# A conditioned decoder layer: the input projection in three rounded products, and key norms taken on strips

## What is computed

```python
h = modulate(x, norm_mix_w, shift1, scale1)
c_q, c_kv, k_rope, slab, gate_a, gate_b = _split(h @ w_in, IN_SIZES)
...
p = p + (prev - p) * rwkv_mu            # prev: the slab of the token before
r, k, v, w_lo, a_lo, g_lo = _split(p, ...)
log_w = -softplus(-(w0 + tanh(w_lo) @ w2)) - 0.5
a = sigmoid(a0 + a_lo @ a2)
g = sigmoid(g_lo) @ g2
kk = heads(k * k_k)
kk = kk / maximum(sqrt(sum(kk * kk, axis=-1)), 1e-12)
k = k * (1.0 + (a - 1.0) * k_a)
```

## Time and profile before

| | us |
|---|---|
| median of three runs | 1730.0 |
| lowest and highest | 1729.05, 1730.19 |
| span of the profiled execution | 1726.8 |
| median less that span | 3.2 |
| `phase_project`, first to last PE matmul | 47.3 to 180.1 |
| the other mixer blocks | 181.2 to about 605 |

### The profile page before, as it was taken

How to read it: one execution, slowest core, us unless ns; L and a number is a source line. 1 busy time by engine, 2 the same in 40 slices (tenths; PEclk the granted TensorE clock), 3 DMA queues, 4 the chain that set the end, 5 groups by cost and what they waited for, 6 DMA issues and landing times.

```text
span 1726.8 us, 44239 instructions
## 1 busy us (share of the span) xinstructions
PE 1664.4 (96%) x18700; PEld 875.8 (51%) x18700; DVE 613.7 (36%) x1421; ACT 412.9 (24%) x849; POOL 279.1 (16%) x349
## 2 busy tenths in 40 slices
PE   8999897899999988999999999999999999999997
PEld 5444796466488973344344344334334434434433
DVE  3679474753234554122122122213213213212212
ACT  3142333555123221121121111111112112112111
POOL 5000530101000011121121221221221221221121
PEclk8999999999999989999999999999999999999999
DMA  9950000401221288999999999999999999999993
GB/s 358 346 206 1 2 5 15 166 1 50 86 109 50 98 310 330 370 395 403 381 408 402 390 401 402 388 398 402 391 393 403 396 390 408 399 389 405 401 361 132
DMA packets 98221, 489.64 MB, mean 284 GB/s; under 512 B 15100, under 2 KB 17209, under 8 KB 48838
## 3 DMA queue, kind: packets, MB, share of 16 engines
q1 hardware_dynamic: 88012, 470.76, 68.9%
q0 software_dynamic: 7504, 16.80, 4.1%
q10 hardware_dynamic: 2636, 1.08, 0.3%
HBM read 478.61 MB, written 19.55 MB: 288 GB/s over the span
## 4 chain that ended last, share of the span: by engine, by line
PE 61%; DVE 1%; issue 0%; ACT 0%; POOLq 0%; DVEq 0%; ACTq 0%
PE bank L2131 38%; PE bank L2142 19%; PE bank L2122 1%; PE bank L2155 1%; PE bank L2143 1%; PE bank L2132 1%; PE bank L2170 0%; PE bank L2165 0%; DVE sb_y L2353 0%; DVE sb_biased L2334 0%; POOLq L2023 0%; ACT sb_xT L2222 0%; DVE sb_bias_part L2367 0%; DVE sb_mod L2344 0%; DVE sb_xT L2324 0%
## 5 line engine op out<-in xcount | busy, mean ns | idle before, releaser
L2131 PE MATMUL bank<-sb_w_raw,sb_xT 128*32 128x512 f32 x4608 | 668.0, 594 | 2.5 <-ACT sb_xT L2222 1.4
L2132 PE MATMUL bank<-sb_w_raw,sb_xT 128*32 128x512 f32 x1536 | 667.5, 594 | 0.0
L2131 PEld LDWEIGHTS bank<-sb_w_raw,sb_xT 128*32 128x32 f32 x4608 | 186.1, 110 | 450.1 <-issue 446.6
L2142 PE MATMUL bank<-sb_w_raw,sb_aT 128*32 128x256 f32 x4608 | 337.9, 379 | 2.0 <-DVE sb_aT L2331 2.0
L2143 PE MATMUL bank<-sb_w_raw,sb_aT 128*32 128x256 f32 x1536 | 337.5, 380 | 0.0
L2334 DVE TENSOR_TENSOR sb_biased<-bank,sb_bias 128x512 f32<-128x512 f32 x96 | 60.3, 683 | 608.8 <-PE bank L2132 537.3
L2142 PEld LDWEIGHTS bank<-sb_w_raw,sb_aT 128*32 128x32 f32 x4608 | 187.7, 110 | 130.8 <-DVE sb_y L2353 2.3
L2233 ACT COPY sb_bias<-sb_last_quarter 32x1536 f32<-32x1536 f32 x32 | 47.0, 1467 | 501.6 <-POOL sb_last_quarter L2290 501.6
L2143 PEld LDWEIGHTS bank<-sb_w_raw,sb_aT 128*32 128x32 f32 x1536 | 166.3, 110 | 0.0
L2132 PEld LDWEIGHTS bank<-sb_w_raw,sb_xT 128*32 128x32 f32 x1536 | 166.2, 110 | 0.0
L2285 POOL TENSOR_TENSOR sb_tick<-sb_ones 128x1 f32<-128x1 f32 x93 | 34.8, 374 | 571.9 <-DVE sb_y L2353 223.2
(11 more groups left out here) (456 smaller groups left out, 2110.5 us busy)
## 6 DMA issues: line engine op xcount, KB each, us to landing
sb_w_raw<-in_w_gate_up_dram SPq DMA_DIRECT2D x256, 1024.0 KB, 17.8
sb_w_raw<-in_w_down_dram SPq DMA_DIRECT2D x128, 1024.0 KB, 19.1
sb_ring<-in_w_in_dram SPq DMA_DIRECT2D x7, 2048.0 KB, 11.1
sb_x<-in_ada_w_dram SPq DMA_DIRECT2D x8, 1024.0 KB, 8.7
sb_mod<-in_ada_w_dram SPq DMA_DIRECT2D x8, 1024.0 KB, 9.1
sb_ring<-in_ada_w_dram SPq DMA_DIRECT2D x3, 2048.0 KB, 12.8
sb_x<-in_x_dram SPq DMA_DIRECT2D x2, 2048.0 KB, 11.0
sb_ring<-in_w_out_dram SPq DMA_DIRECT2D x2, 2048.0 KB, 8.5
```

The source lines that it names most:

```text
L2131: te.matmul(up_bank[r][at, :], g.xT[:, k, at], g.w_raw[:, s, 512 * r:512 * r + 512], start=first, stop=last)
L2132: mm = te.matmul(up_bank[r][CAP:P, :], g.xT[:, k, STRIP * r:STRIP * r + STRIP], g.w_raw[:, s, 512 * G:2048], start=first, stop=last)
L2142: te.matmul(down_bank[j][at, 0:256], g.aT[:, k, at], g.w_raw[:, s, 1024 * r + 256 * j:1024 * r + 256 * j + 256], start=first, stop=last)
```

## The change

The projection's products are made of rounded float32, as the gates' are now. Of `g.hT` and of each weight tile a high part (rounded) and a low part (the rest) are kept, and each product is three: high by high, high by low, low by high.

- `phase_adaln`: hidden features go to `g.h32` (over `g.AR`), the normalised tokens to `g.mod` in place of `xn`. GpSimd, after its constants, splits the first chunk (two copies, two subtractions). SP issues the first two late half chunks here, behind the chunk loads.
- `phase_project`: DVE and ACT round four tiles of the hidden state each; DVE subtracts for the eight low parts. For each of the twelve r, k and v tiles ACT writes the high part into one of three buffers, and GpSimd writes the low part over the raw weights in the ring; ACT and GpSimd do the same for the attention's inputs in one piece of 128 by 3328. The first two outputs do their low-hidden products last.
- Key norms: the sums of squares go to four strips of 32 partitions of one bank (16 matmuls), one square root, one maximum and one reciprocal of 128 by 128, and 16 matmuls spread them back to four banks (rn). ss and rn stand ahead of v in TensorE's list, g behind m. The decays of the first two tiles stand ahead of the norm on DVE.
- `phase_output`: the two ACT casts and two DVE subtractions of `g.hT` go. The low parts, written to DRAM at the end of the projection's SP list, come back by two 1 MB loads, and GpSimd copies them (4 copies of 128 by 1024) before ga.
- Buffers move: `phase_mla` has its v tokens in `g.gate` and its q and k in `g.AR`.

```diff
+def low_slot(g, i):
+
+    k, n = g.chunks[i].shape[1:]
+    return g.ring_r[:, i % RING, 0:k * n].rearrange("p (k n) -> p k n", k=k)
...
+def late_place(g, h):
+    buf = (g.x, g.mod)[h // 2]
+    return buf[:, 2 * (h % 2):2 * (h % 2) + 2, :].rearrange("p a (b n) -> p (a b) n", n=512)
...
+            sp.wait_ge(*act.at(f"xn{NT - 1}"))
+            for h in range(2):
+                sp.dma_start(late_place(g, h), ada_chunk(a, 4, 512 * h, 512 * h + 512)).then_inc(g.late_in[h], 16)
...
+            pool.wait_ge(*chunk_loaded(g, LO))
+            for i in range(2):
+                pool.tensor_copy(g.first_hi[:, i], slot(g, LO)[:, :, P * i:P * i + P]).then_inc(*first(f"hi{i}"))
+            for i in range(2):
+                pool.wait_ge(*first.at(f"hi{i}"))
+                raw = slot(g, LO)[:, :, P * i:P * i + P]
+                pool.tensor_tensor(low_slot(g, LO)[:, :, P * i:P * i + P], raw, g.first_hi[:, i].bitcast(F32), ALU.subtract).then_inc(*first(f"lo{i}"))
...
                 sc.wait_ge(*pe.at(f"h{k}"))
-                sc.activation(g.hT[:, k, :], ps[bank_of[k]][:, :], ACT.Identity, bias=g.mod1_cols[:, k:k + 1], scale=g.gain[:, k:k + 1]).then_inc(*act(f"h{k}"))
+                sc.activation(g.h32[:, k, :], ps[bank_of[k]][:, :], ACT.Identity, bias=g.mod1_cols[:, k:k + 1], scale=g.gain[:, k:k + 1]).then_inc(*act(f"h{k}"))
...
-        squares, norms = flat[:, :, 0:SEQ], flat[:, :, SEQ:2 * SEQ]
+        squares = flat[:, :, 0:SEQ]
...
+            for h in range(2, 4):
+                sp.dma_start(staged[h], ada_chunk(g.a, 5, 512 * h - 1024, 512 * h - 512)).then_inc(late_in[h], 16)
             sp.wait_ge(*vec.at("no_bias"))
-            for h in HALVES:
+            bias(0)
+            bias(1)
...
+            sp.wait_ge(*vec.at(f"hl{KD - 1}"))
+            for i, buf in enumerate(g.low):
+                sp.dma_start(g.h_lo_rows[i], buf[:, :, :].bitcast(F32)).then_inc(g.lo_out, 16)
...
-                    te.wait_ge(*(vec if outs[j - 8] in lerps else act).at(outs[j - 8]))
+                    old = outs[j - 8]
+                    te.wait_ge(*(vec.at(f"kk{old[2]}") if old[:2] == "rn" else (vec if old in lerps else act).at(old)))
...
+            def split(hi, lo, k):
+                return (hi, g.hT[:, k, :]), (hi, g.h_lo[k]), (lo, g.hT[:, k, :])
+
             def feature(name, chunk, i):
-                te.wait_ge(*chunk_loaded(g, chunk))
-                w = slot(g, chunk)
-                product(name, [(w[:, k, P * i:P * i + P], g.hT[:, k, :]) for k in range(KD)])
-
+                n = tiles.index(name)
+                te.wait_ge(*pool.at(f"w{n}"))
+                lo = low_slot(g, chunk)[:, :, P * i:P * i + P]
+                product(name, [x for k in range(KD) for x in split(g.w_hi[:, n % 3, k, :], lo[:, k, :], k)])
+
+            first_lo = [low_slot(g, LO)[:, :, P * i:P * i + P] for i in range(2)]
             for i in range(2):
-                feature(f"l{i}", LO, i)
+                for k in range(KD):
+                    if i == 0:
+                        te.wait_ge(*(act if k % 2 else vec).at(f"hh{k}"))
+                    te.matmul(bank[f"l{i}"][:, :], g.first_hi[:, i, k, :], g.hT[:, k, :], start=(k == 0), stop=False)
+                    te.matmul(bank[f"l{i}"][:, :], first_lo[i][:, k, :], g.hT[:, k, :], start=False, stop=False)
+            for i in range(2):
+                for k in range(KD):
+                    if i == 0:
+                        te.wait_ge(*vec.at(f"hl{k}"))
+                    mm = te.matmul(bank[f"l{i}"][:, :], g.first_hi[:, i, k, :], g.h_lo[k], start=False, stop=(k == KD - 1))
+                mm.then_inc(*pe(f"l{i}"))
...
+            te.wait_ge(*act.at(outs[outs.index("ss") - 8]))
+            for i in f4:
+                te.wait_ge(*act.at(f"sq{i}"))
+                for t in range(NT):
+                    mm = te.matmul(bank["ss"][STRIP * t:STRIP * t + STRIP, 0:P], g.by_head[:, i, :], squares[:, i, P * t:P * t + P], start=(i == 0), stop=(i == FT - 1))
+            mm.then_inc(*pe("ss"))
+            te.wait_ge(*vec.at("rn"))
+            for i in f4:
+                te.wait_ge(*act.at(outs[outs.index(f"rn{i}") - 8]))
+            for r in range(NT):
+                if r:
+                    te.wait_ge(*pe.at(f"rn{r - 1}"))
+                for t in range(NT):
+                    f, at = (t + r) % FT, slice(STRIP * t, STRIP * t + HEADS)
+                    mm = te.matmul(bank[f"rn{f}"][:, P * t:P * t + P], g.from_head[at, f, :], g.rn[at, :], start=True, stop=True)
+                mm.then_inc(*pe(f"rn{r}"))
+            for i in f4:
+                feature(f"v{i}", RKV + 2, i)
+            te.wait_ge(*pool.at("wm"))
+            mla_lo = low_slot(g, MLA)
+            for t in range(NT):
+                at = slice(P * t, P * t + P)
+                product(f"m{t}", [x for k in range(KD) for x in ((g.hT[:, k, at], mla_hi[:, k, :]), (g.hT[:, k, at], mla_lo[:, k, :]),
+                                                                (g.h_lo[k][:, at], mla_hi[:, k, :]))], MLA_IN)
             te.wait_ge(*act.at("sigg"))
             for i in f4:
                 product(f"g{i}", [(g.w_g[:, P * i:P * i + P], g.sg[:, :])])
-            for i in f4:
-                te.wait_ge(*act.at(f"sq{i}"))
-                product(f"ss{i}", [(g.head_ones[:, :], squares[:, i, :])])
-            for i in f4:
-                feature(f"v{i}", RKV + 2, i)
-            te.wait_ge(*chunk_loaded(g, MLA))
-            for t in range(NT):
-                product(f"m{t}", [(g.hT[:, k, P * t:P * t + P], slot(g, MLA)[:, k, :]) for k in range(KD)], MLA_IN)
...
+            def split_hi(n):
+                chunk, i = RKV + n // FT, n % FT
+                sc.wait_ge(*chunk_loaded(g, chunk))
+                if n >= 3:
+                    sc.wait_ge(*pe.at(tiles[n - 3]))
+                sc.copy(g.w_hi[:, n % 3, :, :], slot(g, chunk)[:, :, P * i:P * i + P]).then_inc(*act(f"w{n}"))
+
+            for k in range(1, KD, 2):
+                sc.copy(g.hT[:, k, :], g.h32[:, k, :]).then_inc(*act(f"hh{k}"))
+            for n in range(3):
+                split_hi(n)
             sc.wait_ge(*vec.at("not_mu"))
-            for n in lerps[:6]:
-                own(n)
+            own("l0")
+            own("l1")
+            for i in f4:
+                own(f"r{i}")
+                split_hi(i + 3)
...
+                own(f"k{i}")
+                split_hi(i + 7)
...
-            for i in f4:
-                sc.wait_ge(*pe.at(f"g{i}"))
-                sc.copy(g.gate[:, i, :], bank[f"g{i}"][:, :]).then_inc(*act(f"g{i}"))
-            for i in f4:
-                sc.wait_ge(*pe.at(f"ss{i}"))
-                sc.activation(norms[:, i, :], bank[f"ss{i}"][:, :], ACT.Sqrt).then_inc(*act(f"ss{i}"))
+            sc.wait_ge(*pe.at("ss"))
+            sc.activation(g.rn[:, :], bank["ss"][:, 0:P], ACT.Sqrt).then_inc(*act("ss"))
+            split_hi(11)
+            sc.wait_ge(*chunk_loaded(g, MLA))
+            sc.wait_ge(*pe.at("k3"))
+            sc.copy(mla_hi, slot(g, MLA)).then_inc(*act("wm"))
...
+            sc.wait_ge(g.lo_out, 32)
+            for i in f4:
+                sc.wait_ge(*pe.at(f"g{i}"))
+                sc.copy(g.gate[:, i, :], bank[f"g{i}"][:, :]).then_inc(*act(f"g{i}"))
+
+        @block.gpsimd
+        def _(po):
+            for n in range(len(tiles)):
+                chunk, i = RKV + n // FT, n % FT
+                po.wait_ge(*act.at(f"w{n}"))
+                raw = slot(g, chunk)[:, :, P * i:P * i + P]
+                po.tensor_tensor(low_slot(g, chunk)[:, :, P * i:P * i + P], raw, g.w_hi[:, n % 3, :, :].bitcast(F32), ALU.subtract).then_inc(*pool(f"w{n}"))
+            po.wait_ge(*act.at("wm"))
+            po.tensor_tensor(low_slot(g, MLA), slot(g, MLA), mla_hi.bitcast(F32), ALU.subtract).then_inc(*pool("wm"))
...
+            def hidden_hi(k):
+                ve.tensor_copy(g.hT[:, k, :], g.h32[:, k, :]).then_inc(*vec(f"hh{k}"))
+
+            hidden_hi(0)
+            hidden_hi(2)
+            ve.memset(bias_row, 0.0).then_inc(*vec("no_bias"))
+            hidden_hi(4)
+            hidden_hi(6)
             ve.tensor_scalar(g.not_mu[:, :], g.cols[:, at:at + NMU], -1.0, 1.0, ALU.mult, ALU.add).then_inc(*vec("not_mu"))
-            ve.memset(bias_row, 0.0).then_inc(*vec("no_bias"))
+            for k in range(KD):
+                ve.wait_ge(*(act if k % 2 else vec).at(f"hh{k}"))
+                ve.tensor_tensor(g.h_lo[k], g.h32[:, k, :], g.hT[:, k, :].bitcast(F32), ALU.subtract).then_inc(*vec(f"hl{k}"))
...
-                ve.wait_ge(*act.at(f"ss{i}"))
-                ve.tensor_scalar(g.rn[:, :], norms[:, i, :], 1e-12, None, ALU.max).then_inc(*vec(f"nm{i}"))
-                ve.wait_ge(*vec.at(f"nm{i}"))
-                ve.reciprocal(g.rn[:, :], g.rn[:, :]).then_inc(*vec(f"rn{i}"))
-                ve.wait_ge(*vec.at(f"rn{i}"))
-                ve.tensor_tensor(b, b, g.rn[:, :], ALU.mult).then_inc(*vec(f"kk{i}"))
+            decays(0)
```

(39 more changed lines are left out.)

98 lines of the change are left out of this document (57 added, 41 removed).

## The result

The changed kernel takes 1753.6 us (median of four runs, 1749.5 to 1754.8) against 1729.8: ratio 1.013, 95% interval 1.0111 to 1.015. It is slower by 19 to 26 us. The profiled execution is the fastest of the four, 1749.5, with a span of 1747.7; so in the profile 20.9 us are to be found, and the median has some 3 more. The other three executions show a mean granted clock of 0.970 to 0.974 where the profiled one has 0.977. What lies around a span is 1.8 us in every execution whose own time is known, not 3.2; so the profiled execution of the kernel before took some 1728.6, less than any of its four runs. Four executions of all that follow, of 1925 to 9636 us, stand apart and are left out of every median.

The account below looks back on a forecast made before the run. TensorE bounds the projection, DVE close behind; after the change DVE's list decides. 144.4 (v's start) + 46.7 + 3.3 = 194.4 against 180.1, 14.3 later: 1744.3 us against 1730.0, range 1726 to 1754.

Parts of the forecast that it names:

- The products: TensorE in the projection: rounded products at 0.227 us; ten tiles 54.6 instead of 68.9, v 21.8 instead of 27.5.
- DVE's list and the hold: DVE in the projection: last add at 110.0 unhindered, plus 22 us from eleven GpSimd subtractions of 2.0 each: 132.0.
- sign of eleven adds of 2 to 3 us: Expected in DVE's late adds: average over 1.0 us instead of 0.75, with eleven of 2 to 3 us.
- The waits taken as gone: DVE's late adds: 13.1 us of waits for transfers vanish, as a slower DVE asks for data less often.
- the 110.0 "without hold": DVE in the projection: end of the last late add without any wait, 47.3 + 62.7 us.
- The rival without hold: GpSimd doesn't hold DVE in the projection: block ends at 172.4, 7.7 us earlier, time 1722.3; chance 0.15.
- The chain to v: Projection, last late add to first v product: sigmoids, squares, sums, root, maximum, reciprocal and spread, 12.4 us together.
- The clock behind it: TensorE after its idle gap ahead of v: about 6.6 us at half clock, 3.3 us lost.
- TensorE's list of 46.7: TensorE from v's start to the projection's end: 21.8 + 17.7 + 3.6 + 3.6 us.
- Output block and everything behind at cost 0: Output block: removed casts and subtractions, the reload and GpSimd's copies lie beside TensorE's work, 0 both ways.
- the rival in which both costs add up: DVE in the projection: 25.7 us of hold plus 7.4 of write waits, 11.1 more, 1755; chance 0.06.

Follow-up runs that it names:

- the doubled one: Changed kernel with a second GpSimd subtraction (128 by 896, into an unread buffer) ahead of each of the twelve: one run, 1770.0 us.
- the short pieces: Changed kernel with each of GpSimd's twelve subtractions of 128 by 1024 cut into eight of 128 by 128: one run, 1740.6 us.
- the kernel with small subtractions: Changed kernel with GpSimd's subtraction for each r, k and v weight tile covering 128 columns instead of 1024: ratio 1.0018, median 1737.6 us.
- v early: Changed kernel with DVE doing all weight subtractions, and v0 and v1 right behind k3, ahead of the norm: ratio 0.9997, median 1734.0 us.
- six repeats: Kernel before, with TensorE repeating the projection's last bonus-sum product six times (5.2 us): ratio 1.0070.
- sixteen: Kernel before, with TensorE repeating the projection's last bonus-sum product sixteen times (13.8 us): ratio 1.0104.
- norms alone: Kernel before with only the key norms and the output order changed, products plain float32, GpSimd idle: ratio 1.0074, median 1749.5 us.

## Why the forecast held, and what it missed

*The products* (54.6 for ten tiles, 21.8 for v). Right in kind. They run at 0.231 instead of 0.227, 5.55 a tile and not 5.46, which costs nothing ahead of the late adds and 0.4 us behind. The attention's inputs took 0.190 each and 18.2, forecast 17.7.

*DVE's list and the hold* (110.0 plus 22, last add at 132.0). It ended at 131.2. Each GpSimd instruction took 2.1 from DVE (forecast 2.0), and the doubled one 1.75, or 1.95 with the wait behind it. So the hold was 23.3 and the list without it ended at 107.9: two small errors cancel. My sign of eleven adds of 2 to 3 us was wrong, since only eight instructions meet adds. The Trainium skill ("SBUF — State Buffer", "Summary: rules for kernel authors") says that of a DVE instruction with two SBUF inputs and a GpSimd one that reads SBUF the second to issue is blocked fully until the first is done. For long instructions the trace agrees nearly: 2.1 of 2.4 to 2.5 us, and 5.3 of the 5.5 that the long piece still had to run. For the short pieces it doesn't: an add and a piece pass in 0.8 us, not in 1.2.

*The waits taken as gone.* They were: 2.6 us idle instead of 15.7. But here the forecast hid an error in its rival: the 110.0 "without hold" can't be reached. With hardly any hold the last add ends at 118.2, since the waits come back. The rival without hold was priced at 1722; the kernel with small subtractions took 1.0018 of the kernel before, some 1733.

*The chain to v* (12.4 us). 131.2 to 144.85 is 13.6; the spread ran at half clock, 3.5 instead of 2.3. *The clock behind it* (3.3): that 1.2 and some 1.3 of the first v products, 2.5 together, as the window from 144 to 148 above shows. bo ended at 193.7, forecast 194.4.

*Beside it, unforeseen but free here.* ACT's cast for the last v tile waits for v0 and holds up the exponentials: DVE stood 8.6 us, and then 5.3 more for GpSimd's long piece. TensorE's list of 46.7 covered both. With v early they had to be taken out.

*Output block and everything behind at cost 0.* This is the step that failed: 13.6 of the 20.9 us come from the projection, 7.3 from behind it, and the median has 3 more. The reload and GpSimd's copies did lie hidden, as I said. What I left out is that moving the later blocks in time has a price in this kernel even for blocks whose code is the same: by the ratios 8 us with six repeats, and 3 to 4 with sixteen and with norms alone, which is hardly more than the noise. Neither nor anything else that I used prices it, and its cause is open for the greater part.

So the mechanism in the projection held, and the number held by luck. 1753.6 lies outside the 1739 to 1749 to which I gave 0.68, and 0.4 us inside the edge of the whole range. It is nearest to the rival in which both costs add up (1755), and that one is wrong: the waits that it adds were gone.
